# A two-layer streaming encoder step on one core: residual passages reordered, rotary rows of four query heads in one tile, new latents turned inside the prompt heads

## What is computed

```python
def layer(x, pos, p, lb, kv_past, pe_past, past_pos, S0, conv_buf, is_prompt):
    h = rmsnorm(x, p['norm_mix_pre'])
    mix, kv_lat, k_pe, S_new = token_mixers(h, pos, p, lb, kv_past, pe_past, past_pos, S0, is_prompt)
    x = x + rmsnorm(mix, p['norm_mix_post'])
    h = rmsnorm(x, p['norm_ffn_pre'])
    f, buf = conv_ffn(h, p, conv_buf)
    x = x + rmsnorm(f, p['norm_ffn_post'])
    return x, kv_lat, k_pe, S_new, buf
```

## Time and profile before

| | |
|---|---|
| median of 3 runs | 1989.63 us (1988.48 to 1989.74) |
| profiled execution, its own time | 1987.55 us |
| its span, first to last instruction | 1985.7 us |
| mean granted TensorE clock | 0.983 of full |
| TensorE busy | 1896.6 us, 96% |
| VectorE busy | 1129.3 us, 57% |
| ScalarE busy | 761.1 us, 38% |
| GpSimd busy | 114.4 us, 6% |
| moved by transfers | 141.8 MB, 71 GB/s on average |

### The profile page before, as it was taken

One profiled execution on the slowest core, in us unless ns is written; L12 is line 12 of the kernel. 1 busy time (PEld: TensorE's weight loads), 2 busy tenths in 40 slices (PEclk: granted clock), 3 DMA queues, 4 the chain that ended last, 5 costly groups with the idle time before them and its releaser, 6 DMA issues.

```text
span 1985.7 us, 30228 instructions
## 1 busy us (share of the span) xinstructions
PE 1896.6 (96%) x12028; PEld 1738.2 (88%) x12028; DVE 1129.3 (57%) x1807; ACT 761.1 (38%) x1207; POOL 114.4 (6%) x117
## 2 busy tenths in 40 slices
PE   7999989999999999999999999899989999999996
PEld 6999865588899999999889998655989999999994
DVE  5677874434766316663467778544257661366535
ACT  5444545435422222223454444454354222222235
POOL 0000033300000000000000001331000000000000
PEclk9999999999999999999999999899999999999998
DMA  4211120321122221212121111304112222212111
GB/s 179 75 55 66 55 67 32 113 73 54 57 86 75 75 75 64 85 64 76 56 96 44 55 66 54 88 22 133 54 43 79 75 71 79 75 65 82 69 63 59
DMA packets 45116, 141.82 MB, mean 71 GB/s; under 512 B 5472, under 2 KB 11488, under 8 KB 44960
## 3 DMA queue, kind: packets, MB, share of 16 engines
q1 hardware_dynamic: 37280, 121.58, 17.9%
q10 hardware_dynamic: 7696, 18.30, 2.7%
HBM read 130.13 MB, written 8.65 MB: 70 GB/s over the span
## 4 chain that ended last, share of the span: by engine, by line
PE 77%; DVE 12%; ACT 7%; DMA 2%; issue 2%; ACTq 0%; SPq 0%; DVEq 0%
PE G L429 63%; PE WA L429 8%; PE WB L429 3%; DVE wlo L1420 2%; DVE tmp L1420 2%; ACT sq L960 1%; DVE X L1420 1%; PE G L433 1%; PE WB L433 1%; DVE Y L1420 1%; ACT whi L960 1%; ACT Hh L960 1%; DVE Z L1420 1%; DVE Hl L1420 1%; DMA Y<-in_qrows 1%
## 5 line engine op out<-in xcount | busy, mean ns | idle before, releaser
L429 PE MATMUL G<-Hh,wlo 128*128 128x328 f32 x2144 | 688.9, 321 | 30.2 <-DVE Hl L1420 27.4
L429 PE MATMUL G<-Hh,whi 128*128 128x328 f32 x2144 | 674.7, 315 | 0.0
L429 PE MATMUL G<-Hl,whi 128*128 128x328 f32 x2144 | 669.3, 312 | 0.0
L429 PEld LDWEIGHTS G<-Hh,wlo 128*128 128x128 f32 x2144 | 406.3, 189 | 46.1 <-DVE Hl L1420 32.9
L429 PEld LDWEIGHTS G<-Hh,whi 128*128 128x128 f32 x2144 | 405.5, 189 | 1.6 <-issue 0.2
L429 PEld LDWEIGHTS G<-Hl,whi 128*128 128x128 f32 x2144 | 405.9, 189 | 0.0
L960 ACT ACTIVATE whi<-wraw 128x1024 fp32r<-128x1024 f32 x192 | 203.6, 1060 | 513.0 <-PE G L429 490.5
L1420 DVE TENSOR_TENSOR wlo<-wraw,whi 128x1024 fp32r<-128x1024 f32 x192 | 235.3, 1226 | 235.8 <-ACT whi L960 226.4
L429 PE MATMUL G<-gl,whi 128*128 128x328 f32 x704 | 220.4, 313 | 0.0
L429 PE MATMUL G<-gh,wlo 128*128 128x328 f32 x704 | 220.2, 313 | 0.0
L429 PE MATMUL G<-gh,whi 128*128 128x328 f32 x704 | 219.6, 312 | 0.0
(11 more groups left out here) (243 smaller groups left out, 2423.9 us busy)
## 6 DMA issues: line engine op xcount, KB each, us to landing
wraw<-in_wstream SPq DMA_DIRECT2D x192, 512.0 KB, 3.2
ckT<-in_ckT SPq DMA_DIRECT2D x12, 512.0 KB, 4.0
ctok<-in_ctok SPq DMA_DIRECT2D x12, 512.0 KB, 3.3
S<-in_s ACTq DMA_DIRECT2D x8, 512.0 KB, 5.9
o_sst<-S ACTq DMA_DIRECT2D x8, 512.0 KB, 2.9
o_y<-Y SPq DMA_DIRECT2D x16, 164.0 KB, 1.8
ckT<-in_ckT ACTq DMA_DIRECT2D x4, 512.0 KB, 3.8
ctok<-in_ctok ACTq DMA_DIRECT2D x4, 512.0 KB, 3.8
```

The lines of the kernel that those rows point to most:

```text
L429: return pe.matmul(out, lhsT, rhs, start=start, stop=stop, skip_group_check=True)
```

## The change

**Passages.** `split_xh` is taken apart: ScalarE's copies to `Hh` and its squares are placed one by one, the `Hh` of a block ahead of the squares of earlier blocks, and the pieces `w_high` and the squares and copies of the last output tiles lie between them in a new order. On VectorE the residual of the next pair comes ahead of the `Hl` of the last one. In `first_two` half 0 of the third tile starts after block 4 of half 0 (in layer 0's first passage it stays where it was), waits for that bank by itself (`third_free`), and is done after block 3 of half 1. The sum of squares of the last blocks (`norm_sum`) comes after block 4 in all passages.

The diff, cut to its core:

```diff
-Q_ORDER = [0, 1, 2, 3, 6, 7, 5, 4]
+Q_NOPE = {2: (0, 1), 3: (2, 3), 6: (6, 7), 7: (4, 5)}
...
+        sin4 = sb(hg, "sin4", [P, T])
+        q_turned = gate[:, 0, :]
...
+        def by_kind(t, p, turned):
...
+            v = t.rearrange("p (h k c) -> p h k c", h=4, k=2)
+            return [v[:, :, :, 0:NOPE]] + [v[:, :, k, NOPE:P].rearrange("p h (s c) -> p h s c", s=2) for k in range(2)]
...
-                if g % PIECES == P_OUT + 4:
+                if g % PIECES == P_OUT + 3:
 
                     l = g // PIECES
-                    sp.wait_ge(S("o"), HG * (l + 1))
+                    for half in range(2):
+                        sp.wait_ge(S("roped"), 2 * l + half + 1)
+                        if half:
+                            sp.wait_ge(S("o"), HG * (l + 1))
+                        for i in range(4):
+                            sp.dma_start(Y[64:96, 4 * half + i, :], q_turned[32 * i:32 * i + 32, :]).then_inc(S("q_rope"), 16)
                     sp.wait_ge(S("dec"), HG * (l + 1))
+                    sp.wait_ge(S("kpe"), l + 1)
                     sp.dma_start(KT[64:96, :, :], kpe[64:96, 0:PT].rearrange("p (a n) -> p a n", a=1)
                                  .broadcast_to([ROPE, HM, PT])).then_inc(S("maskrows"), 16)
                     sp.dma_start(KT[96:100, :, :], a["krows"]).then_inc(S("maskrows"), 16)
                     sp.dma_start(Y[96:100, :, :], a["qrows"]).then_inc(S("maskrows"), 16)
+                    sp.wait_ge(S("o_taken"), HG * (l + 1))
+                    sp.wait_ge(S("q_rope"), 128 * (l + 1))
+                    sp.dma_start(cpe[0:NOPE, 0, :], a["wB"][l]).then_inc(S("wB_in"), 16)
...
+            def finish_kpe(l):
+
+                tt = l * TILES + T_LAT + 3
                 pool.wait_ge(S(f"evac{tt % 2}"), slot_use(tt))
-                pool.tensor_tensor(Y[64:96, h, :], Y[64:96, h, :], tmp[64:96, i % 2, :], ALU.add)\
-                    .then_inc(S("rotated"), 1)
-                pool.wait_ge(S("rotated"), l * HM + i + 1)
+                pool.tensor_tensor(kpe[64:96, :], kpe[64:96, :], tmp[64:96, 0, :], ALU.add).then_inc(S("kpe_sum"), 1)
+                pool.wait_ge(S("kpe_sum"), l + 1)
+                pool.tensor_tensor(kpe[64:96, :], kpe[64:96, :], R[64:96, :], ALU.mult).then_inc(S("kpe"), 1)
+
+            def add_turned(l, half):
+
+                tt = l * TILES + T_UQ + 4 * half + 1
+                pool.wait_ge(S(f"evac{tt % 2}"), slot_use(tt))
+                pool.wait_ge(S("q_products"), 2 * l + half + 1)
+                if half:
+                    pool.wait_ge(S("q_rope"), 128 * l + 64)
+                pool.tensor_tensor(q_turned, tmp[:, 0, :], tmp[:, 1, :], ALU.add).then_inc(S("roped"), 1)
...
                         between(x, k)
-                        if x:
-                            half_tile(tt + 2, [(g + 2, c * P, c) for c in range(KD)], Hh, Hl, 0, (k, k + 1), None)
-                half_tile(tt + 2, [(g + 2, c * P, c) for c in range(KD)], Hh, Hl, 1, (0, KD), "tile")
+                        if halves_free is None:
+                            if x:
+                                third(0, k)
+                        elif KD // 2 <= KD * x + k < KD // 2 + KD:
+                            third(0, KD * x + k - KD // 2)
+                for k in range(KD):
+                    third(1, k)
...
+                e = tr(G[1][0:DT, 3 * P:4 * P], kvn[:, PT + DT * h:PT + DT * h + DT])
                 e.then_inc(S("turned"), 1)
...
                 keys(1)
                 pe.wait_ge(S("s0_new"), l * HG + HG)
                 square_sum(n0 + N_HG[HG - 1], 0, WB)
-                keys(2)
+                pe.wait_ge(S("wB_in"), 16 * (l + 1))
+                for i in (6, 7):
+                    pe.wait_ge(S(f"evac{(t0 + T_UQ + i) % 2}"), slot_use(t0 + T_UQ + i))
+                tile_free(t0 + T_UK + 2)
+                for h in range(HM):
+                    e = mm(G[1][:, P * h:P * h + P], cpe[0:NOPE, 0, P * h:P * h + P], Y[0:NOPE, h, PT:T])
+                e.then_inc(S("ql_ps"), 1)
                 pe.wait_ge(S("maskrows"), 48 * (l + 1))
                 keys_taken(0)
                 keys_taken(1)
                 prompt_scores(l, 0)
+                pe.wait_ge(S("ql"), l + 1)
+                keys(2)
                 values(0)
                 values(1)
-                keys(3)
+                prompt_scores(l, 1)
                 values(2)
                 values(3)
...
                 def q_nope(i):
-                    tt, h = t0 + T_UQ + i, Q_ORDER[i]
+                    tt = t0 + T_UQ + i
                     act.wait_ge(S("tile"), tt + 1)
-                    did(f(two(Y[0:64, h, :]), halves(G[tt % 2], p1=64), ACT.Copy, scale=SCALE), "q_nope")
+                    for h in Q_NOPE[i]:
+                        p0 = NOPE * (h % 2)
+                        e = f(two(Y[0:NOPE, h, :]), halves(G[tt % 2], p0=p0, p1=p0 + NOPE), ACT.Copy, scale=SCALE)
+                        if p0:
+                            evac(tt, e)
+                        else:
+                            step(e)
 
...
+                out_b_square(KD - 3)
+                w_high(l, P_UP[0])
+                high(0, 0)
+                square(0, 0)
+                w_high(l, P_UP[0] + 1)
+                high(0, 1)
+                high(0, 2)
+                out_b_copy(KD - 3)
+                out_b_square(KD - 2)
+                square(0, 1)
+                w_high(l, P_UP[0] + 2)
+                high(0, 3)
+                square(0, 2)
+                high(0, 4)
+                out_b_square(KD - 1)
+                out_b_copy(KD - 2)
+                square(0, 3)
+                square(0, 4)
+                high(0, 5)
+                square(0, 5)
+                rstd_post_b(2 * l + 1)
+                high(0, 6)
+                square(0, 6)
+                high(0, 7)
...
+                    rstd_end(0)
+                    for k in range(4):
+                        square(1, k)
+                    scale_out(0, 0)
+                    scale_out(0, 1)
+                    for k in range(4, KD):
+                        square(1, k)
+                    act.dma_start(a["o_conv"][l], cout[:, :, :]).then_inc(S("conv_out"), 16)
+                    rstd_end(1)
...
-                def queries(i):
-                    h = Q_ORDER[i]
-                    dve.wait_ge(S("q_nope"), l * HM + i + 1)
-                    if i >= 2:
-                        dve.wait_ge(S("rotated"), l * HM + i - 1)
-                    rotate(t0 + T_UQ + i, Y[64:96, h, :], SCALE, i % 2)
+                def turn_queries(half):
+
+                    if half:
+                        dve.wait_ge(S("roped"), 2 * l + 1)
+                    else:
+                        dve.wait_ge(S("kpe"), l + 1)
+                    for i, table in ((0, cos4), (1, sin4)):
+                        tt = t0 + T_UQ + 4 * half + i
+                        dve.wait_ge(S("tile"), tt + 1)
+                        evac(tt, stt(two(tmp[:, i, :]), halves(G[tt % 2]), SCALE, two(table[:, :]), ALU.mult, ALU.mult))
...
                 residual(0, 0)
+                add_square_b(n0 + N_MIXPOST, KD - 3)
                 residual(0, 1)
                 rest(0, 0)
                 residual(0, 2, 2)
                 w_low(l, P_UP[0])
+                w_low(l, P_UP[0] + 1)
                 rest(0, 1)
-                add_square_b(n0 + N_MIXPOST, KD - 3)
-                w_low(l, P_UP[0] + 1)
+                residual(0, 4, 2)
                 rest(0, 2)
                 rest(0, 3)
-                residual(0, 4, 2)
+                rest(0, 4)
                 add_square_b(n0 + N_MIXPOST, KD - 2)
-                rest(0, 4)
+                w_low(l, P_UP[0] + 2)
                 rest(0, 5)
                 add_square_b(n0 + N_MIXPOST, KD - 1)
                 residual(0, 6, 2)
                 rest(0, 6)
+                dve.wait_ge(S("rstd"), n0 + N_MIXPOST + 1)
+                residual(1, 0)
                 rest(0, 7)
-                dve.wait_ge(S("rstd"), n0 + N_MIXPOST + 1)
-                dve.wait_ge(S(f"evac{(t0 + T_OUT + KD - 1) % 2}"), slot_use(t0 + T_OUT + KD - 1))
-                residual(1, 0)
...
+            def out_a(k):
+
+                dve.wait_ge(S("rstd_end"), 1)
+                did(tt_(Y[:, k:k + 2, cols_of(0)], X[:, k:k + 2, cols_of(0)], spread(0, 2), ALU.mult), "y_raw", by=2)
+
+            out_a(0)
+            residual(1, 4, 2)
+            scaled_b()
+            residual(1, 6, 2)
+            out_a(2)
+            out_a(4)
+            out_a(6)
+            dve.wait_ge(S("rstd_end"), 2)
+            for k in range(KD):
                 did(stt(Y[:, k, cols_of(1)], X[:, k, cols_of(1)], col(0, C_FIN + k), R[:, cols_of(1)],
                         ALU.mult, ALU.mult), "y_out")
 
```

349 lines of the change are left out of this document (199 added, 150 removed).

## The result

| | before | changed |
|---|---|---|
| median of 14 runs each | 1989.68 us (1978.45 to 1995.9) | 1998.81 us (1992.58 to 2007.81) |
| ratio to before | | 1.0048, 95% interval 1.0025 to 1.0071 |
| profiled execution, its own time | 1987.55 us | 1996.90 us |
| its span, mean granted clock | 1985.7 us, 0.983 | 1995.1 us, 0.974 |

The change makes the kernel slower by 0.5%. The forecast was 1971.3 us, faster, in 1958 to 1984: wrong in sign, and the time lies outside the range.

A forecast was written before the change was run, and what follows sets the result against it. TensorE, busy 1896.6 of 1985.7 us, was taken as the bound, leaving only its idle time and low clock to win. 8.4 + 7.4 + 2.0 - 1.5 + 0 - 1 + 3 = 18.3 us gave 1971.3 us, range 1958 to 1984.

The forecast's parts named there:

- Passages from mixing to feed-forward: Where the mixing result enters the residual: reordered Hh copies and third tile save 4.2 us each, 8.4 us for two.
- My sign: Expected evidence in the profile after: TensorE's waits for Hl fall from 28.1 to under 10 us.
- Passage between the layers: From 976.02 to 1017.16 us, 10.0 us lost; TensorE starts 1.4 us later, loses 1.2 more, 7.4 us saved.
- The end: Last 30 us: earlier norm sum and final scaling shared by ScalarE and VectorE, 2.0 us gained.
- sin: Start of each layer: loading sin4 (328 KB) costs 0.95 us in layer 0, half in layer 1; 1.5 us lost.
- Rotary rows and keys: End of the HGRN heads to the first prompt turn: savings and the wait for wB balance, 0 us.
- The lock: VectorE operations beside GpSimd's additions at level 6 lose 2.4 us in all, between nothing and 3.1.
- the lower sum: 1972.7 us: the sum if VectorE operations just after GpSimd's wait their whole length, twice, at the shared port.
- The 7 us wait for wB: TensorE arrives at 280.3 us and stands 7 us before ql; wB lands at 287.5, bounded by 283 and 290.
- The clock: Low clock after gaps near 299.8 and 1271 us cost 1.4 and 8.8; charged 3.6 per layer, 3 us gained.
- Rival (c): After the 7 us wait TensorE runs at half speed for 8.8 us instead of 3.6, twice: 1981.7 us; chance 0.09.
- Rival (d): Row copies take 10.5 us a group instead of 2.5, 1997.7 us; sign: wait before ql over 12 us; chance 0.04.

The follow-up runs named there:

- e1: The kernel before with only the three passages changed, old end kept; 1982.16 us, ratio 0.9960.
- e3: The kernel before with the passages and the end changed, nothing else; 1979.04 us, ratio 0.9938.
- e4: The changed kernel with sin's four loads issued by ScalarE at the end of head 1 instead of the layer's start; 1993.78 us, ratio 1.0028.
- e14: The changed kernel with sin's four loads issued by GpSimd instead of ScalarE at the same moment; 2000.59 us, ratio 1.0061.
- e5: The changed kernel with the rotary key's last two steps (addition and product) back on VectorE instead of GpSimd; 1993.65 us, ratio 1.0024.
- e12: The changed kernel without the second group of four row copies, so four heads lack their rotary rows; 1992.96 us, ratio 1.0022.
- e6: The changed kernel with wB's load issued by ScalarE again, after the first two keys' copies and the rotary rows' landing; 2002.28 us, ratio 1.0080.
- e7: The changed kernel with 64 unread identity matmuls ahead of TensorE's wait for wB; 2000.38 us, ratio 1.0041.
- e10: The changed kernel with 34 unread identity matmuls ahead of TensorE's wait for wB; 1988.69 us, ratio 1.0010.
- e9: e3 with 7, 3, 6 and 9 unread identity matmuls in four of TensorE's waits of each last head; 1968.67 us, ratio 0.9907.

## Why the prediction was wrong

The forecast had 18.3 us gained, and the profiled execution lost 9.4. By the table of delays the difference lies in these stretches: the passages gave 12.8 us for 15.8 forecast, the end lost 1.1 for 2.0 gained (the old end lost 1.0 in e1's profile too), the starts of the layers lost 6.7 for 1.5, and from head 2 to the first prompt scores 12.6 and 12.5 us were lost, where I had 4.9 a layer. Behind those scores 10.7 came back, where I had 11.7: 9.7 up to the first turns, and 2 from the clock less the turns of the new latents.

**Passages from mixing to feed-forward, 8.4 us forecast: right**, 4.1 and 3.8 by the timeline, with the part that comes back at the fifth tile (0.4 of the 1.1 I took). My sign, waits for Hl under 10 us, did not come (13.0), since I hadn't set apart the 10.3 of the program's start.

**Passage between the layers, 7.4: mis-sized**, 4.9. I took 1.4 us for the later start; TensorE stood 2.60 us, and ran at the low clock behind it. And "the chain behind it (gates of head 0) hangs on the fourth tile and moves with TensorE" was wrong: it hangs on a weight load as well, so that another 1.8 us are gone over the first head (e3).

**The end, 2.0: nothing.** The second residual half came 1.5 us sooner, as forecast (1970.22 on a timeline 8.3 us late, against 1963.38). But VectorE now scales half 0 between the residuals of half 1, and the squares that feed the last norm wait for it: that norm is 1.5 us later than the timeline's 8.3. No run takes this order apart from the rest of the end.

**sin, -1.5: a third of it.** It costs 4.5 us by the timeline (e4: 2.8 and 1.7) and 5.0 by the medians, by its transfers (e14). I had the kind of cost right and priced 328 KB at 350 GB/s in layer 0 and half of that in layer 1. And the four issues, which I let fall into slack, took ScalarE until the weight piece went out 1.8 us later; it then landed the faster, so they add nothing (e14).

**Rotary rows and keys, 0 us: the first step that failed.** The lock was well priced: 2.4 us forecast from the kvn row, 1.44 + 1.17 us measured, and both gone in e5 (it struck the weight part and the first product, not two products). The Trainium skill's rule for that port (SBUF — State Buffer, the pair shared by VectorE and GpSimd) is borne out as a mechanism: each VectorE operation lost what was left of GpSimd's. GpSimd's own product, 2.43 us where I had 1.57, fits a wait for the weight part. A whole length each time, as I read the rule for the lower sum, would have asked for 3.1. The split of a query piece, which I priced at 0.45 us more, took 0.32 more on VectorE, as the sum in my own bracket gives, and 0.40 on ScalarE.

The 7 us wait for wB was well sized too (8.2 and 8.4). What I got wrong is where the row copies stand. I let SyncE begin them at 273.5 and wB land by 290 at the latest; it began at 281.8, because they wait for the last head's output, which came 7.6 us late instead of 1.0 early, and wB landed at 296.4. The four issues ahead of it cost 2.5 us a layer (e12). And between level 6 and the last output another 2.6 us went, though the gaps there are fewer (1.42 us instead of 3.8): the clock was at 0.68 and 0.66 for ten microseconds each, and I had priced only the gap.

Of my reading of wB's place behind the others one thing fell: the queue hardly matters, since wB takes 8.4 us from its issue on a queue of its own (e6) and 9.2 behind the others, with the DMA engines busy for 0.96 of the time. What the Trainium skill says of increments landing behind earlier writes (DMA: Bandwidth & Descriptors, queues, rings and completion order) is not needed for that wait; no run here shows it by itself.

**The clock, +3 us gained: the step that turned the sign.** I took the low clock of before as something the change would mostly remove, by 3.6 us a layer left of 1.4 and 8.8. In the profile the clock falls at each of the three gaps, 3.5, 1.4 and 8.2 us. Behind the wait for wB it does so in every run that leaves that wait open; behind the 1.4 us gap not always (in layer 0 of e7, the same up to there, it stays up). Held up at the wB wait alone, it gives back 10.1 us (e10), more than the 9.1 by which the change is slower. The Trainium skill (TensorE: Matmul & The Clock Gate, HAM oscillation) tells of just this, a wait for a transfer between two stretches of matmuls that sends the engine back to half clock each time; the trace agrees, 0.57 over the 20 us around the wait and 1.00 with it filled.

Rival (c) had the mechanism, at 0.09, on one wait instead of three; no rival had the late head. Rival (d), 1997.7 us, came within 1.1 us of the measured time by luck: its slow copies didn't happen (a group took 2.4 us to issue, and each copy landed 2.1 us after its issue), and the wait stayed at 8.2, under its sign of 12. The profile of before was also read as if its clock were a property of the kernel: in its layer 0 the clock fell for about 7 us only behind the turns of the new latents, where in e1 and e3, the same there, it fell for 20. In e1 this scatter hid half of what the passages gained.

## What to carry to other kernels

A wait on TensorE costs its own length and then the low clock behind it, so a change that takes many small gaps away and makes one of 8 us can lose (here 10.1 us of clock for two such waits); price the clock with every gap that a change makes. Read the clock of each stretch before taking one profiled execution as the kernel: where executions scatter, put time against mean clock for each of them and compare at an equal clock. Where a wait can't be removed, useless matmuls in it, no more than the wait holds, are worth trying: here they gave 8.5 to 10 us and took most of the scatter away (with as few as 6 executions in e9). Check what the filler itself takes first.

## What was not expected of the hardware

TensorE's granted clock went to 0.50, the 1.2 GHz level, after gaps as short as 1.4 to 3.5 us in some executions and not in others. In e3's profile gaps of 1.81, 0.70 and 1.77 us were followed by a clock of 0.52 and 0.50 from 265 to 275 us; the profile of before has the same gaps, one of 1.29 us more, and a clock of 1.00 there. The kernel before, unchanged, runs from 1976 to 2005 us, and its time follows the mean clock (correlation -0.98). A matmul of a float32 identity by itself, 128 columns, took 0.23 us and two records in the trace (128 for 64 matmuls in e7), where a turn of the same size took one of 0.11.
